# Roots of the norms applied behind the projections of two feed-forwards, keys, queries and values

## The reference

```python
def rms_norm(x, g, eps=NORM_EPS):
    y = xf * lax.rsqrt(jnp.mean(xf * xf, axis=-1, keepdims=True) + eps)
    return (y * g.astype(jnp.float32)).astype(x.dtype)

def swiglu_ffn(h, w_gu, w_down):
    gate, up = jnp.split(h @ w_gu, 2, axis=-1)
    return (jax.nn.silu(gate) * up) @ w_down
...
    k, v = jnp.split(rms_norm(x, kv_g) @ kv_w, 2, axis=-1)   # shared keys and values
    q = (rms_norm(x, g_mix[1]) @ w_q)                        # queries of layer 1
    x = x + swiglu_ffn(rms_norm(x, g_ffn[layer]), w_gu, w_down)   # both layers
```

## Time and profile before

| | us |
|---|---|
| median of 3 runs | 1399.5 (1395.93 to 1400.88) |
| profiled execution | 1391.34 |
| its span | 1389.3 |

### The profile page before, as it was taken

How to read it: one execution, slowest core, us unless ns; L and a number is a source line. 1 busy time by engine, 2 the same in 40 slices (tenths; PEclk the granted TensorE clock), 3 DMA queues, 4 the chain that set the end, 5 groups by cost and what they waited for, 6 DMA issues and landing times.

```text
span 1389.3 us, 21888 instructions
## 1 busy us (share of the span) xinstructions
PE 1253.1 (90%) x9218; PEld 1165.7 (84%) x9218; DVE 937.6 (67%) x1294; ACT 634.1 (46%) x835; POOL 206.5 (15%) x139
## 2 busy tenths in 40 slices
PE   4998988989899999699878889999789887999995
PEld 3887878777899999696658888999789877999995
DVE  6767566554478874646864666874558835999994
ACT  4464343253543445555555565434433234544442
POOL 0000000000454441000000111210000002344431
PEclk9999999899899999899998999999899998999998
DMA  7441001001676654253223677875333213555530
GB/s 270 146 162 33 32 1 62 1 1 48 244 250 247 243 183 152 93 186 115 98 89 119 212 267 269 292 276 183 109 138 113 74 57 121 183 170 184 185 130 31
DMA packets 122656, 200.26 MB, mean 144 GB/s; under 512 B 3264, under 2 KB 111168, under 8 KB 112320
## 3 DMA queue, kind: packets, MB, share of 16 engines
q1 hardware_dynamic: 117664, 168.11, 35.8%
q0 software_dynamic: 3456, 25.17, 4.8%
q10 hardware_dynamic: 1440, 5.60, 1.1%
HBM read 197.82 MB, written 1.05 MB: 143 GB/s over the span
## 4 chain that ended last, share of the span: by engine, by line
PE 64%; DVE 24%; ACT 7%; issue 4%; DMA 0%; DVEq 0%; POOL 0%; ACTq 0%
PE bank L638 13%; PE bank L639 12%; PE bank L640 12%; DVE buf L2453 7%; DVE ring_r L1760 6%; PE bank L721 3%; PE bank L723 3%; PE bank L722 3%; ACT high L1211 3%; PE bank L901 2%; DVE work L2029 2%; PE bank L654 2%; DVE work L2025 2%; PE bank L889 2%; PE bank L1103 1%
## 5 line engine op out<-in xcount | busy, mean ns | idle before, releaser
L638 PE MATMUL bank<-part,high 128*128 128x256 f32 x1664 | 486.8, 293 | 58.9 <-DVE part L1767 51.1
L1760 DVE TENSOR_TENSOR ring_r<-ring,high 128x2048 fp32r<-128x2048 f32 (+1 forms) x155 | 343.8, 2227 | 205.8 <-ACT high L1211 203.5
L639 PE MATMUL bank<-part,high 128*128 128x256 f32 x1664 | 481.7, 290 | 0.0
L640 PE MATMUL bank<-part,ring_r 128*128 128x256 f32 x1664 | 481.2, 289 | 0.0
L638 PEld LDWEIGHTS bank<-part,high 128*128 128x128 f32 x1664 | 330.9, 199 | 66.0 <-issue 41.9
L639 PEld LDWEIGHTS bank<-part,high 128*128 128x128 f32 x1664 | 331.0, 199 | 1.3 <-issue 1.2
L640 PEld LDWEIGHTS bank<-part,ring_r 128*128 128x128 f32 x1664 | 330.7, 199 | 0.0
L1211 ACT ACTIVATE high<-ring 128x2048 fp32r<-128x2048 f32 x155 | 295.1, 1906 | 51.1 <-PE bank L640 40.9
L1687 POOL TENSOR_TENSOR ring_r<-ring,high 128x512 fp32r<-128x512 f32 x44 | 92.7, 2107 | 523.4 <-ACT high L1211 523.3
L721 PE MATMUL bank<-part,high 128*128 128x256 f32 x528 | 151.3, 286 | 9.2 <-POOL part L1681 4.9
L722 PE MATMUL bank<-part,high 128*128 128x256 f32 x528 | 150.1, 284 | 0.0
(11 more groups left out here) (267 smaller groups left out, 1568.5 us busy)
## 6 DMA issues: line engine op xcount, KB each, us to landing
ring<-in_wide SPq DMA_DIRECT2D x122, 1024.0 KB, 5.9
ring<-in_down SPq DMA_DIRECT2D x33, 1024.0 KB, 4.9
buf<-in_wide POOLq DMA_DIRECT2D x24, 1024.0 KB, 7.2
con<-in_cons SPq DMA_DIRECT2D x1, 1536.0 KB, 11.1
ring<-in_wide SPq DMA_DIRECT2D x2, 576.0 KB, 7.0
buf<-in_wide ACTq DMA_DIRECT2D x1, 1024.0 KB, 5.1
buf<-in_wide SPq DMA_DIRECT2D x1, 1024.0 KB, 5.2
buf<-in_ctx_t ACTq DMA_DIRECT2D x1, 1024.0 KB, 7.3
```

What stands on the lines that cost most here:

```text
L638: mm(bank, ah, bh, start=start, stop=False, skip_group_check=shared)
L639: mm(bank, ah, bl, start=False, stop=False, skip_group_check=shared)
L640: return mm(bank, al, bh, start=False, stop=stop, skip_group_check=shared)
L1760: v.tensor_tensor(low, raw, hi.bitcast(F32), ALU.subtract).then_inc(sem("unit_low"), 1)
```

## The change

The root of norms 1 (first feed-forward), 3 (keys, queries, values) and 4 (second feed-forward) is no longer multiplied into the activation ahead of the projection, but into its result. What is split is residual x weight alone: ACT writes the high part straight from `resid` with the weight column as scale (`gained_high`), DVE the low part in one instruction (`gained_low`). `norm_apply` is gone.

PE takes the sums of these norms behind the first unit of the projection that follows. In the feed-forward, DVE multiplies each bank (gate and up) by the root into SBUF (`scale_both`, frees the bank), ACT takes Silu of the gate there, in place, and DVE multiplies gate and up (`gated_scaled`), for tile f-1 behind the scaling of tile f; ACT's `gate_high` follows one tile later as well. The last `gated_scaled` stands behind the loop. Keys and queries are multiplied out of their banks by DVE in place of ACT's copy; for values PE turns the root (two transposes), ACT copies two columns of it to `root_tok`, and the copy out of the bank takes it as scale. The context's norm 2 keeps its way, with a root tile of its own (`rstd_c`), as `rstd` is in use for the whole feed-forward. Bank places are set so that the moved sums find a free bank. The third feed-forward keeps its instructions.

```diff
-        place(("norm", 1))
+        place_at(("norm", 1), 0)
...
                         close(unit_columns(bank, w, f"ffn{n}", c + i == 0), key)
+                        if c + i == 0 and n < 2:
+                            norm((1, 4)[n])
...
-                norm(3)
-                project("ak", "hkv")
+                project("ak", "hkv", lambda: norm(3))
                 project("aq", "hq")
...
+                bank = open_bank(("root_turned", 0))
+                pe.wait_ge(sem("norm_root"), 4)
+                for t in range(TT):
+                    last = nc.tensor.transpose(bank[:, t * P:(t + 1) * P], rstd[:, t * P:(t + 1) * P], ident)
+                close(last, ("root_turned", 0))
                 tokens("av", 0, [("av", 0), ("av", 1)], "hkv", False)
...
+                def gained_high(name, j):
+                    for kt in (2 * j, 2 * j + 1):
+                        ins = act_(high_of(name)[:, kt, :], resid[:, kt, :], ACT.Identity, scale=pcol(GAINS[name], kt))
+                        ins.then_inc(sem("part_high"), 1) if kt % 2 else own.go(ins)
...
                 def ffn(n, between=lambda c: None):
                     for f in range(FT):
-                        key = ("gu", n, f)
-                        wait_full(eng, key)
-                        if f >= 4:
-                            wait_freed(eng, ("gu", n, f - 4))
-                        act_(gate_tmp(f), bank_of(key)[:, 0:S], ACT.Silu).then_inc(sem("gate"), 1)
+                        if f == 0:
+                            root((1, 4)[n])
+                        wait_freed(eng, ("gu", n, f))
+                        gate = scaled(f)[:, 0, :]
+                        act_(gate, gate, ACT.Silu).then_inc(sem("gate"), 1)
                         ahead(f"gu{n}", f // 2, f % 2)
-                        gate_high(n, f)
+                        if f:
+                            gate_high(n, f - 1)
                         if f % 2:
                             between(f // 2)
                             if f // 2 >= LAG:
                                 ahead(f"dn{n}", f // 2 - LAG, 0)
+                    gate_high(n, FT - 1)
...
-                def project_resid(name, norm_no):
+                def project_resid(name, norm_no, into=None):
                     log_table()
                     for j in range(4):
                         wait_freed(eng, (name, j))
+                        if into:
+                            gained_high(into, j)
                         square(norm_no, resid, j)
...
+                def gained_low(name, j):
+                    eng.sem_inc(sem("part_raw"), 1)
+                    eng.wait_ge(sem("part_high"), part_value(name, j))
+                    for kt in (2 * j, 2 * j + 1):
+                        ins = v.scalar_tensor_tensor(low_of(name)[:, kt, :], resid[:, kt, :], pcol(GAINS[name], kt), high_of(name)[:, kt, :].bitcast(F32),
+                                                     ALU.mult, ALU.subtract)
+                        ins.then_inc(sem("part_low"), 1) if kt % 2 else own.go(ins)
...
+                def scale_both(n, f):
+                    key = ("gu", n, f)
+                    wait_full(eng, key)
+                    release(v.tensor_tensor(scaled(f), bank_of(key)[:, :].rearrange("p (a n) -> p a n", a=2), spread(rstd[:, :], [P, 2, S]), ALU.mult), key)
+
+                def gated_scaled(n, f):
+                    eng.wait_ge(sem("gate"), FT * n + f + 1)
+                    wait_act_slot(eng, n, f)
+                    v.tensor_tensor(act_value(f), scaled(f)[:, 0, :], scaled(f)[:, 1, :], ALU.mult).then_inc(sem("act_raw"), 1)
+
+                def ffn(n, between=lambda c: None):
                     norm_root((1, 4)[n])
-                    norm_apply(resid, f"ffn{n}", lambda kt: pcol(gname, kt))
                     for f in range(FT):
+                        scale_both(n, f)
+                        if f >= 1:
+                            gated_scaled(n, f - 1)
                         ahead(f"gu{n}", f // 2, f % 2)
-                        gated(n, f, slice(S, 2 * S))
                         between(f)
                         if f % 2 and f // 2 >= LAG:
                             ahead(f"dn{n}", f // 2 - LAG, 0)
+                    gated_scaled(n, FT - 1)
...
-                down_resid(0, plain_add)
-                norm_root(3)
-                norm_apply(resid, "hkv", lambda kt: pcol("kv_g", kt))
+                down_resid(0, plain_add, lambda j: gained_low("hkv", j - 1) if j else None)
+                gained_low("hkv", 3)
                 down_ahead(0)
-                norm_apply(resid, "hq", lambda kt: pcol("g_mix1", kt))
+                for j in range(4):
+                    gained_low("hq", j)
```

More of the change, by code:

```diff
@@ L178, in build @@
         rstd = sb("rstd", [P, S])
+        rstd_c = sb("rstd_c", [P, S])
         tiny = sb("tiny", [P, 640])
@@ L310, in build @@
             unit_job("o", i // 2, i % 2, ("o", i))
-        place(("norm", 1))
+        place_at(("norm", 1), 0)
         plan_ffn(0, lambda c: [("norm", 2)] if c == 10 else ())
+        place(("ak", 0))
         place(("norm", 3))
-        plan_proj("ak")
+        for i in range(1, 4):
+            place(("ak", i))
+        for i in range(4):
+            unit_job("ak", i // 2, i % 2, ("ak", i))
         plan_proj("aq")
@@ L318, in build @@
                 place((n, j))
+        place(("root_turned", 0))
         plan_tokens("av", 0, [("av", 0), ("av", 1)])
@@ L348, in build @@
         plan_proj("awo")
-        place(("norm", 4))
+        place_at(("norm", 4), 0)
         plan_ffn(1, lambda c: [("csum", d, t) for d in range(2) for t in range(TT)] if c == 4 else
@@ L1244, in proj_out, with tokens_out @@
                         ahead(name, j // 2, j % 2)
-                def tokens_out(stage, c, keys, dst):
+                def tokens_out(stage, c, keys, dst, scale=lambda t: 1.0):
                     ahead(stage, c, 0)
@@ L1249, in tokens_out @@
                         wait_full(eng, keys[t])
-                        release(act_(dst(t), bank_of(keys[t])[:, :], ACT.Copy), keys[t])
+                        if stage == "av":
+                            ins = act_(dst(t), bank_of(keys[t])[:, :], ACT.Identity, scale=scale(t))
+                        else:
+                            ins = act_(dst(t), bank_of(keys[t])[:, :], ACT.Copy)
+                        release(ins, keys[t])
                     ahead(stage, c, 1)
@@ L1466, in project_resid @@
                             ahead(name, j // 2, j % 2)
-                    root(norm_no)
-                project_resid("o", 1)
-                parts("ffn0")
+                    if not into:
+                        root(norm_no)
+                project_resid("o", 1, "ffn0")
                 ahead("o", 1, 1)
@@ L1488, in context_norm @@
                         log_table()
-                        root(2)
+                        root(2, rstd_c)
                 ffn(0, context_norm)
@@ L1805, in down_resid @@
                         release(ins, key) if cb % 2 else own.go(ins)
+                        if cb % 2:
+                            after(cb // 2)
                     for j in range(KT // 2):
@@ L2123, in gain_of, with modulated @@
                                                     pcol(g, 0, 8).unsqueeze(2), ALU.add, ALU.mult))
-                def modulated(src, name, i, which, part):
+                def modulated(src, name, i, which, part, root=rstd):
                     for j in range(4):
                         for kt in (2 * j, 2 * j + 1):
-                            own.go(v.scalar_tensor_tensor(value_of(name)[:, kt, :], src[:, kt, :], gain[:, 8 * i + kt:8 * i + kt + 1], rstd[:, :],
+                            own.go(v.scalar_tensor_tensor(value_of(name)[:, kt, :], src[:, kt, :], gain[:, 8 * i + kt:8 * i + kt + 1], root[:, :],
                                                           ALU.mult, ALU.mult))
```

83 lines of the change are left out of this document (47 added, 36 removed).

## The result

The changed kernel takes 1416.4 us (median; 1409.74 to 1422.99) beside 1400.2 for the kernel before (1395.93 to 1401.15): ratio 1.0122, 95% interval 1.0069 to 1.0174, so it is slower by 1.2%. Timed again beside the experiments it gave 1.0143 (1.0117 to 1.0169).

The account below looks back on a forecast made before the run. TensorE, busy nine tenths of the span, was taken to bound the kernel. Second key unit +2.5, values +0.5 and second feed-forward +9.3 gave +12.3 on a 1399.5 median: 1412 us, range 1389 to 1427.

Parts of the forecast that it names:

- First norm, -5.5: At the first feed-forward's start: the next unit starts at 365.7 instead of 371.2 us, 5.5 us gained.
- a short one nothing: On PE's clock: a long gap costs about 2.4 us on top of itself, a short gap adds no low-clock cost.
- First loop, +15.3: First feed-forward: serial scaling, Silu, high and low parts make pairs 18.85 against PE's 17.25 us; 9.6 plus 5.7 lost.
- The lag before tile 7: First feed-forward: the chain falls behind after tiles 2 and 3, so PE loses 5.7 us waiting for a later unit.
- rival (b): VectorE and GpSimd hold each other up more in the loop: 12 to 16 us more, 1426 us; chance 0.13.
- Keys, -7.3: From down unit 8's end to the second key unit: pieces are ready without the root, +28.0 instead of +35.3 us.
- rival (d): At the norms: the first unit waits just as long for gained pieces, so no gains, 1431 us; chance 0.03.
- Values and second norm, +0.5 - 6.6: Keys, queries and values lose 0.5 us to transposes and small copies; the norm before the second feed-forward gains 6.6.
- Second loop, +8.8: Second feed-forward: the context gates' block costs 3.9 us more, further waits behind it 4.4, and 0.5 later.
- its end, +7.1: Second feed-forward's end: the late last gating product makes PE idle 4.8 us, plus 2.3 of low clock, with nothing covering it.
- (a): The feed-forward loop hides the added chain, if a modulation takes under 5.3 or ACT isn't held: -9, 1390 us; chance 0.16.
- (c): Nothing to measure: DVE's idle absorbs lags, the end wait is shorter, gains and losses cancel, 1399 us; chance 0.11.

Follow-up runs that it names:

- e6: The kernel before with the change made for keys, queries and values alone, both feed-forwards as before; ratio 0.9931 to the kernel before.
- e1: The changed kernel with ACT making the high part of the unit three ahead before Silu's wait in both changed feed-forwards; ratio 0.9894 to the kernel before.
- after_again: The changed kernel unaltered, timed and profiled again beside the experiments; ratio 1.0143 to the kernel before.
- e2: The changed kernel with the last gating product and its high part ahead of the split that waits for down unit 8, both changed feed-forwards; ratio 1.0101 to before.
- e3: The changed kernel with the edits of both e1 and e2; ratio 0.9849 to the kernel before.
- e7: e3 plus, in the output projections, ACT making the high part of the coming weights before it waits for the residual; ratio 0.9765 to the kernel before.
- e5: The kernel before with one more, unused DVE product of bank and root per tile in the first two feed-forwards; ratio 1.0047 to the kernel before.

## Why the prediction was right, and where it was short

Direction, mechanisms and places hold; the size is 20 us from the mark (16 by the first median), where I had 12.3. At the sums behind the second feed-forward 8.9 are missing: 2.4 at the first norm, 2.5 in the first loop and 7.0 in the second with its end, against which the stretch from keys to the second feed-forward came out 2.9 better than forecast, most of it by luck of the one trace. By its steps:

- **First norm, -5.5, measured -3.1.** PE reached the first unit within 0.3 us of when I said and waited 2.72 instead of 2.2. What I left out is the clock behind it. The prediction took it that a long gap costs 2.4 us more "and a short one nothing"; a window of PE in after shows 24 matmuls in 4.4 us, at a granted clock of 0.61, nearer the lower level (1.2 GHz), after 2.72 of idle:

```profile
365.80:370.20 4.40, 4.40 (x24) 0.61 0.95 377
```

 They cost some 1.5 more than at full clock. The step that failed is the word "nothing", and the trace of before had it already: a clock of 0.64 behind its wait of 2.70 at 346.12. And the same wait in e6, at 346.15, leaves the clock at 1.00. Windows of PE, before and then e6:

```profile
346.20:351.00 4.80, 4.80 (x28) 0.64 1.06 349
```

```profile
346.20:351.00 4.80, 4.80 (x40) 1.00 1.03 344
```

 So no length of idle parts the two cases here. The loop shows it too: of the once-a-pair waits, those at 458, 477 and 497 leave the clock at 1.00, and the one at 516.11, just as long, has 0.60 behind it. Windows of PE in after, behind the waits at 496.84 (1.76) and at 516.11 (1.75):

```profile
497.00:501.20 4.20, 4.20 (x36) 1.00 0.67 242
516.10:520.30 4.20, 4.19 (x23) 0.60 0.52 217
```

 Where the pair's period is DVE's, a low clock costs nothing more: it only uses up the next wait, which is 0.29 behind the spell at 516.
- **First loop, +15.3, measured +17.8.** The lag before tile 7 was 5.32 of idle; I said 5.7. The pair was 19.26 instead of 18.85, and six pairs lose 2.0 each instead of 1.6. The difference is rival (b) in small: the down unit's low part takes 2.92 where I put 2.29 (its row is in the earlier trace rows; the 2.29 in rows 6 is an idle), because POOL's quarter, begun at 455.39, runs on to 458.22 when it starts at 457.46; the modulation takes 6.7, not 6.9. I had looked for the pair's wait behind DVE's low part; it is POOL's quarter that ends last, as shown above. Timeline of POOL in the same pair, and the groups of its gated low part (count, busy us and mean ns), first after, then before:

```profile
458.19 2.78 POOL L1718 TENSOR_TENSOR part<-buf,part 128x256 fp32r<-128x256 f32 x1
...
L1718 POOL TENSOR_TENSOR part<-buf,part 128x256 fp32r<-128x256 f32 x66 | 139.0, 2107 | 236.9 <-ACT part L1296 236.9
```

```profile
L1681 POOL TENSOR_TENSOR part<-buf,part 128x256 fp32r<-128x256 f32 x66 | 100.0, 1517 | 224.6 <-ACT part L1266 224.6
```

 The same subtraction costs 2.1 us instead of 1.5 on average. Most of that is in the second feed-forward (1.14 in before, 2.45 in after, and 2.05 in e1, which has `gate_high` one tile later as well): there it starts behind a low part of DVE and runs beside it. The new gating product was the place where I feared for contention, and it was hardly hit (0.41 and 0.42 above, 0.45 on average over all 44). The Trainium skill, "SBUF — State Buffer", Who interferes with whom, states that VectorE instructions with two SBUF inputs contend with GpSimd instructions that read SBUF. The trace agrees: the low part that starts while POOL is at work takes 2.92; one of the second feed-forward that starts at 863.39, 0.36 ahead of POOL's subtraction, takes 2.29, and the subtraction takes 2.51, where it is 0.74 alone. The product escaped only by its place in time.
- **Keys, -7.3.** From the end of down unit 8 to the second key unit it is 7.4 us less than before, and 7.4 less in e6, which has the part alone. There, without the wait behind POOL, rival (d)'s wait for the gained pieces is seen (4.50).
- **Values and second norm, +0.5 - 6.6.** Together -9.0 in after and -7.0 in after_again. Most of the 2.0 between them is clock, not the change: from 713 to 715 after_again runs at a granted clock of 0.51, where after has 1.00, and in the 4.5 us behind the wait for the attention's output projection it has 0.51 and after 0.68. The other five traces with all three moves come to between -6.0 and -6.4, so the forecast of -6.1 was good and after's own -9.0 is luck.
- **Second loop, +8.8, and its end, +7.1: measured 22.9 together.** The gates' block cost 7.59 of idle (7.8 said), the two waits behind it 1.64 and 1.78 (2.4 and 1.7 said). The term that was mis-sized is the last wait of the sum, 1.8: the context's sums need a free bank, which DVE's scaling (L1870) now frees, and DVE is late there: 4.93 where before has 1.49 behind its gating product. Behind it PE runs 5.5 us at a granted clock of 0.50. Against before that is 3.4 of idle and some 2.7 of clock, 6.1 of the 7.0 that are missing in this step.
- The gained activation took 0.50 on average (L1255 in after, 32 of them), where I took 0.45; a difference that the prediction priced at 0.2 us in all.
- One more thing the steps left out: a wait costs PE 0.24 more than its idle in the timeline (pair 19.26 - 17.25 = 2.0 for an idle of 1.76), because a matmul of 0.28 normally has the next one start 0.12 behind its own start, and the first behind the wait has its next one 0.19 behind it: 0.16 and 0.07. With six waits in the first loop that is some 1.4 us, and it is in the 2.0 per pair above.

**The rivals.** (a), that the loop hides, needed a modulation under 5.3 or an ACT that isn't held: it was 6.7, and e1 shows that the second condition alone gives the rival's sign and more. (b) was there at 0.4 per pair, not 1.5. (c) did not come, and of (d) only the wait at keys that e2, e3, e6 and e7 show (4.5).

## What to carry to other kernels

When a step moves from one engine's input to another engine's result, look at what stands behind the new wait in each list: work that is already ready (here a high part of 1.9 us) must come before it, and the same change goes from 20 us lost to 21 us gained without one instruction more (e3). Compare the cycle of the chain, not the busy time, with what the bounding engine needs; after and e1 have the same load on DVE (963.6 and 965.3 us busy) and are 34 us apart. And price the stages where a bank is freed by the moved step as well as those where its result is used.

## What the runs showed of the hardware that was not expected

The granted clock fell to between 0.50 and 0.62 near 308 to 325 us in eight of eleven traces (not in before, e2 and e6), in programs that are the same up to there. The mark lies at 324.22 in before and at 333.33 in e5, whose window is this:

```profile
308.00:325.00 17.00, 17.00 (x57) 0.50 0.00 0
```

PE was busy throughout it, and no trace shows what begins it. It is as large as half the effects studied here, so a single span is compared from a mark behind it. Behind the mark, too, the same wait is followed by a low clock in one trace and not in another: behind 1.75 us of idle at 476.20 after_again has 0.59, where after, in the same place at 477.59, stays at 1.00.
